# Smaller expert blocks, quarter rows and a third weight slot in a routed decoder layer

## What is computed

```python
def hier_moe(h, w_grp, b_grp, w_exp, b_exp, we_gate, we_up, we_down):
    g_sel = argmax(h @ w_grp + b_grp)                  # one of 4 groups
    top_v, top_i = top_k((h @ w_exp + b_exp)[g_sel], 2)  # two of its 8 experts
    ...
    # rows sorted by expert, padded into blocks; per block of rows xb of expert e:
    #   (silu(xb @ we_gate[e]) * (xb @ we_up[e])) @ we_down[e]
    return segment_sum(y * weight, token)
x = layer_norm(ALPHA * x + g1 * mix, ln1_g, ln1_b)
hf = modulate(x, sh2, sc2)
x = layer_norm(ALPHA * x + g2 * hier_moe(hf, ...), ln2_g, ln2_b)
```

## Time and profile before

| | us |
|---|---|
| median of 3 runs (lowest to highest) | 1522.08 (1512.19 to 1526.45) |
| span of the profiled execution | 1523.0 |
| TensorE busy in it | 1262.4 (83%) |
| VectorE busy | 413.6 (27%) |
| ScalarE busy | 307.3 (20%) |
| bytes moved by DMA | 307.24 MB, 202 GB/s in the mean |

### The profile page before, as it was taken

How to read it: one execution, slowest core, us unless ns; L and a number is a source line. 1 busy time by engine, 2 the same in 40 slices (tenths; PEclk the granted TensorE clock), 3 DMA queues, 4 the chain that set the end, 5 groups by cost and what they waited for, 6 DMA issues and landing times.

```text
span 1523.0 us, 18481 instructions
## 1 busy us (share of the span) xinstructions
PE 1262.4 (83%) x6402; PEld 815.4 (54%) x6403; DVE 413.6 (27%) x704; ACT 307.3 (20%) x433; POOL 127.0 (8%) x203
## 2 busy tenths in 40 slices
PE   3899999999999999999987379798887977788710
PEld 3687878787878888888643223233332332233300
DVE  3326240423332260010386601111111111111156
ACT  3255550410000320000100012121211111111221
POOL 0100000000000000000000111111111111111134
PEclk9899999998878999999998579999998999889965
DMA  8744412124232213413003457996999999999631
GB/s 286 238 171 157 176 56 69 48 72 151 83 110 70 84 56 114 165 56 111 31 15 155 193 194 299 389 348 262 396 397 379 393 367 394 383 378 391 259 119 55
DMA packets 69930, 307.24 MB, mean 202 GB/s; under 512 B 10039, under 2 KB 18744, under 8 KB 56917
## 3 DMA queue, kind: packets, MB, share of 16 engines
q1 hardware_dynamic: 59786, 294.77, 50.5%
q0 software_dynamic: 6272, 10.14, 2.1%
q10 hardware_dynamic: 3820, 1.60, 0.4%
HBM read 298.35 MB, written 18.55 MB: 208 GB/s over the span
## 4 chain that ended last, share of the span: by engine, by line
PE 64%; DMA 18%; DVE 8%; issue 4%; ACT 3%; SPq 2%; ACTq 0%; POOL 0%; POOLq 0%; DVEq 0%; PEldq 0%
PE ps L1482 33%; DMA mem<-in_we_up 13%; PE ps L1750 12%; PE ps L1759 5%; PE ps L1709 3%; DMA mem<-in_w_mod 2%; PE ps L1639 2%; PE ps L1742 2%; PE ps L1636 1%; PE ps L1621 1%; DVE mem L1445 1%; PE ps L1647 1%; DMA mem<-in_we_gate 1%; DVE mem L1444 1%; PE ps L1515 1%
## 5 line engine op out<-in xcount | busy, mean ns | idle before, releaser
L1482 PE MATMUL ps<-mem 128*128 128x260 f32 (+1 forms) x2336 | 546.6, 396 | 10.3 <-ACT mem L813 3.9
L1482 PEld LDWEIGHTS ps<-mem 128*128 128x128 f32 (+1 forms) x2336 | 454.5, 196 | 95.3 <-issue 12.6
L1750 PE MATMUL ps<-mem 128*64 128x512 f32 x1120 | 286.7, 671 | 99.9 <-DMA mem<-in_we_up 78.4
L1750 PEld LDWEIGHTS ps<-mem 128*64 128x64 f32 x1120 | 89.7, 154 | 270.9 <-issue 270.9
L1424 DVE TENSOR_TENSOR mem<-mem,ps 64x512 f32<-64x512 f32 x35 | 24.1, 690 | 431.3 <-ACT mem L1002 431.3
L1759 PE MATMUL ps<-mem 128*64 128x512 f32 x560 | 129.2, 604 | 3.4 <-issue 3.4
L1002 ACT ACT_TABLE_LOAD x35 | 44.9, 1283 | 372.5 <-PE ps L1750 372.5
L1759 PEld LDWEIGHTS ps<-mem 128*64 128x64 f32 x560 | 37.5, 138 | 66.8 <-issue 64.5
L710 POOL DMA_INDIRECT pair_scratch<-mem x35 | 32.7, 934 | 458.2 <-DVE mem L1416 458.2
L1416 DVE COPY mem<-ps 64x512 f32<-64x512 f32 x70 | 48.1, 688 | 78.1 <-PE ps L1759 77.0
L1709 PE MATMUL ps<-mem 128*128 128x512 f32 x128 | 59.8, 628 | 0.0
(11 more groups left out here) (284 smaller groups left out, 988.7 us busy)
## 6 DMA issues: line engine op xcount, KB each, us to landing
mem<-in_we_gate SPq DMA_DIRECT2D x32, 2048.0 KB, 12.0
mem<-in_we_up SPq DMA_DIRECT2D x32, 2048.0 KB, 16.5
mem<-in_we_down SPq DMA_DIRECT2D x32, 2048.0 KB, 8.9
mem<-in_w_in SPq DMA_DIRECT2D x14, 2048.0 KB, 8.5
mem<-in_w_mod SPq DMA_DIRECT2D x12, 2048.0 KB, 12.0
out<-mem SPq DMA_DIRECT2D x13, 512.0 KB, 5.3
mem<-in_state_gla SPq DMA_DIRECT2D x8, 512.0 KB, 3.9
mem<-v_scratch SPq DMA_DIRECT2D x8, 512.0 KB, 4.3
```

The lines of the kernel that those rows point to most:

```text
L1482: ins = pe.matmul(out[0:m, h, 0:HALF], w[:, k, col:col + m], src[:, k, h * HALF:(h + 1) * HALF], start=(k == 0), stop=(k == KD - 1))
L1750: ins = pe.matmul(ps[CAP * q:CAP * q + CAP, 2 + j, :], xT[j][:, k, :], ring[3 * slot + q][:, k, :], start=(k == 0), stop=(k == KD - 1))
```

## The change

- `CAP` goes from 64 to 32 rows per block, the largest number of blocks from 48 to 64. A block's rows lie as quarter rows: partition 32 q + s holds values 256 q to 256 q + 255 of row s. Gather and scatter move 128 quarter rows of 1 KB, with an index for each, instead of 64 rows of 4 KB.
- With 32 stationary columns, gate_up writes four column groups: two halves of gate, two halves of up, each 256 wide. down likewise writes four quarters of the result. The row transposes become 2 of 128 x 128, the activation transposes 2 of 64 x 128, the result copy one of 128 x 256. The routing table is made in four column groups.
- The values of `hf` are stored in a permuted order (so the routing weights are loaded in that order too).
- Weights have three slots (`SLOTS`). To make room, buffers are laid out anew: the matrices of the slots lie at `UNITS`, over memory that the first half has done with. Expert 0 is loaded right after job `pb` 7, gate and up of expert 1 after the last `wo` product, then its down matrix, gate and up of expert 2 when the last logits are done, its down matrix when the first two gathers have landed. In the loop expert n waits for expert n-3.
- The plan has for each block its slot and one load count (two register loads, not three), and TensorE branches over three slots. The register loads stand ahead of the block's waits.
- `ln1_g` and `ln1_b` are loaded by SP just after the modulation rows, not by ACT after `z_ready`; `ln2_g`, `ln2_b` and g2 by POOL after the first two gathers. ACT preloads the table of silu ahead of the loop.

```diff
-CAP = 64
+CAP = 32
+QT = P // CAP
+QD = D // QT
+SLOTS = 3
...
-NBLK = 48
+NBLK = 64
...
-SPLITS = 9
+SPLITS = 17
+UNITS = ((0, 3, 4), (1, 2, 6), (7, 8, 5))
...
-        ring = [area(s * WT, KD, 512) for s in range(6)]
+        ring = [area(s * WT, KD, 512) for s in range(9)]
...
-            sp.dma_start(mod_sb[0:NS, 2 * D:6 * D], mod_dram[0:NS, 2 * D:6 * D]).then_inc(mod_back, 16)
+            sp.dma_start(mod_s[0:NS].rearrange("p v d -> p (v d)"), mod_dram[0:NS, 2 * D:5 * D]).then_inc(mod_back, 16)
+            for v, name in enumerate(("ln1_g", "ln1_b")):
+                sp.dma_start(lnp[:, v, :], t[name][0:1, :].to_broadcast([P, D])).then_inc(lnp_in, 16)
...
-                to = ring[3 * slot + m]
+                to = ring[UNITS[slot][m]]
...
-                    sp.dma_start(to.rearrange("p k n -> p (k n)"), w.rearrange("o (p k) n -> p (o k n)", p=P))\
-                      .then_inc(we_in[3 * slot + m], 16)
+                    sp.dma_start(to.rearrange("p (h a) n -> p h (a n)", h=2),
+                                 w.rearrange("o (h p c) n -> p (o h) (c n)", h=2, c=2)).then_inc(we_in[3 * slot + m], 16)
...
+            sp.wait_ge(job_done, INDEX[("pb", 7)] + 1)
+            for m in range(3):
+                load_expert(0, m, 0)
+            sp.wait_ge(outs_ready, 1)
...
             sp.wait_ge(job_done, INDEX[("wo", ORDER[4])] + 1)
-            load_expert(0, 0, 0)
-            load_expert(0, 1, 0)
-            load_expert(0, 2, 0)
             load_expert(1, 0, 1)
+            load_expert(1, 1, 1)
             store_hf(4)
+            load_expert(1, 2, 1)
+            sp.wait_ge(out_sem, 16 * 4)
+            load_expert(2, 0, 2)
             sp.wait_ge(job_done, INDEX[("lg", ORDER[4])] + 1)
-            load_expert(1, 1, 1)
+            for j in range(2):
+                sp.wait_ge(hf_out[j], 16 * (3 - j))
+            load_expert(2, 1, 2)
             sp.wait_ge(blocks_ready, 1)
             for j in range(2):
                 sp.wait_ge(xg_in[j], 16)
-            load_expert(1, 2, 1)
+            load_expert(2, 2, 2)
...
-                pool.indirect_dma_start(xg[j][0:CAP, :], None, hf_dram,
-                                        bass.IndirectOffsetOnAxis(ap=gidx[j][0:CAP, 0:1], axis=0),
+                pool.indirect_dma_start(xg[j], None, hf_dram.rearrange("t (q d) -> (t q) d", q=QT),
+                                        bass.IndirectOffsetOnAxis(ap=gidx[j][:, 0:1], axis=0),
...
+            sc.preload_act_table(ACT.Silu)
...
-                h = hf[p % 2][0:r, :]
-                link(normalise(h, x, r))
-                link(v.tensor_tensor(h, h, modvec(2, i), ALU.mult))
-                link(v.tensor_tensor(h, h, modvec(1, i), ALU.add))
+                h = hf[p % 2][0:r, :].rearrange("t (k p) -> t p k", k=KD)
+                by_k = lambda a: a.rearrange("t (p k) -> t p k", k=KD)
+                link(normalise(u, x, r))
+                link(v.tensor_tensor(u, u, modvec(2, i), ALU.mult))
+                link(v.tensor_tensor(h, by_k(u), by_k(modvec(1, i)), ALU.add))
...
+                for q in range(QT):
+                    ins = pe.matmul(out[CAP * q:CAP * q + CAP, 0, 0:2 * NBLK], place_oh[0:r, n, :],
+                                    named[0:r, n].rearrange("p b c -> p (b c)"),
+                                    start=(n == 0), stop=(n == 2 * TILES - 1))
...
+                for c in range(2):
+                    ins = pe.transpose(ps[:, j, c * P:(c + 1) * P], xg[j][:, c * P:(c + 1) * P], ident[:])
...
                 for k in range(KD):
-                    for q in range(2):
-                        ins = pe.matmul(ps[CAP * q:CAP * q + CAP, 2 + j, :], xT[j][:, k, :], ring[3 * slot + q][:, k, :],
-                                        start=(k == 0), stop=(k == KD - 1))
+                    for q in range(QT):
+                        w = ring[UNITS[slot][q // 2]]
+                        ins = pe.matmul(ps[CAP * q:CAP * q + CAP, 2 + j, 0:QD], xT[j][:, k, :],
+                                        w[:, k, (q % 2) * QD:(q % 2 + 1) * QD], start=(k == 0), stop=(k == KD - 1))
...
-                lies, in0, in1 = weights_of(i * 2 + j)
-                pe.wait_ge(we_in[2], in0 * 16)
-                pe.wait_ge(we_in[5], in1 * 16)
-                for slot in range(2):
-                    with pe.If(lies < 1 if slot == 0 else lies > 0):
+                pe.wait_ge(y_ready[j], i + 1)
+                for slot in range(SLOTS):
+                    with pe.If(lies == slot):
+                        pe.wait_ge(we_in[3 * slot + 2], turn * 16)
                         down(j, slot)
```

More of the change, by code:

```diff
@@ L210, in build @@
         rms = [area(TB + 2080 + NT * j, NT) for j in range(2)]
[L211 to L223, removed]
+        mod_s = area(6 * WT, 3, D)
+        lnp = area(6 * WT + 3072, 2, D)
+        bc = area(A0, 3, D)
+        hf = [area(A0 + 3072 + 1024 * j, D) for j in range(2)]
+        hfT = [area(A0 + 5120 + 1024 * j, KD, P) for j in range(2)]
+        lt = area(A0 + 7168, D)
+        U = 9 * WT
+        X0 = Z0 + 4160
+        x_tok = area(X0, TILES, D)
+        g2b = area(U, D)
+        ln2 = area(U + 1024, 2, D)
+        xg = [area(U + 3072 + QD * j, QD) for j in range(2)]
+        xT = [area(U + 3584 + QD * j, KD, CAP) for j in range(2)]
+        sg = [area(U + 4096 + QD * j, QD) for j in range(2)]
+        act = [area(U + 4096 + QD * j, QD) for j in range(2)]
+        acT = [area(U + 4608 + P * j, 2, 2, CAP) for j in range(2)]
+        yb = [area(U + 4864 + QD * j, QD) for j in range(2)]
+        assert U + 6336 == X0
         yp = [area(WT + 2048 * i, 2, D) for i in range(TILES)]
         ft = [area(4 * WT + 1024 * j, D) for j in range(TILES)]
-        small = [Z0 + 4160]
+        small = [X0 + TILES * D]
         def keep(*shape):
@@ L264, in build @@
         scan_mask = area(2 * WT + 3080, NT)
-        v_samp = area(2 * WT, D)
         v_samp = keep(D)
+        g2s = v_samp
+        q_base = keep(1)
         rt = [TB]
@@ L293, in build @@
         hits = rtmp(NE)
-        plan_f = rtmp(5)
+        plan_f = rtmp(4)
+        load_no = rtmp(1)
         plan_i = rtmp(6).bitcast(I32)
-        row = rtmp(2)
+        row = rtmp(3)
+        turns = rtmp(10)
         place_no = rtmp(CAP)
@@ L308, in build @@
         iota_i = rtmp(64)
[L312 to L322, removed]
+        idx = area(U + 5376, TW, 2).bitcast(I32)
+        gidx = [area(U + 5508 + j, 1).bitcast(I32) for j in range(2)]
+        sidx = [area(U + 5510 + j, 1).bitcast(I32) for j in range(2)]
+        plan = area(U + 5512, 4 * NBLK + 4).bitcast(I32)
+        BLK_SLOT, BLK_TURN, LD_EXPERT, LD_AFTER = (k * NBLK for k in range(4))
+        N_BLK, N_LD, N_EVEN, N_ODD = (4 * NBLK + k for k in range(4))
+        place_oh = area(U, 2 * TILES, CAP)
+        block_oh = area(U + 320, 2 * TILES, NBLK)
+        named = area(U + 960, 2 * TILES, NBLK, 2)
+        outrow = [area(TB + 2944, D), area(A0 - 1024, D)]
         job_done = sem("job_done")
@@ L403, in build @@
         pair = lambda name: [sem(f"{name}{j}") for j in range(2)]
-        we_in = [sem(f"we_in{s}") for s in range(6)]
+        we_in = [sem(f"we_in{s}") for s in range(3 * SLOTS)]
         gidx_copied = sem("gidx_copied")
@@ L960, in _ @@
             sc.wait_ge(z_ready, KD)
-            for v, name in enumerate(("ln1_g", "ln1_b")):
-                sc.dma_start(lnp[:, v, :], t[name][0:1, :].to_broadcast([P, D])).then_inc(lnp_in, 16)
             await_job(sc, ("wo", 4))
@@ L1386, in _ @@
-            for k in range(2):
-                link(v.tensor_scalar_add(plan_i[:, 2 + k:3 + k], plan_i[:, 0:1], 2 + k))
-            link(v.tensor_single_scalar(plan_i[:, 4:6], plan_i[:, 2:4], 1, ALU.logical_shift_right))
-            link(v.tensor_copy(plan_f[:, 1:3], plan_i[:, 4:6]))
+                link(v.tensor_reduce(into, hits[:], AX, ALU.add))
+            link(v.tensor_scalar_min(plan_f[:, 2:3], plan_f[:, 2:3], float(NE - 1)))
+            link(v.scalar_tensor_tensor(hits[:, 0:10], turns[:], load_no[:, 0:1], ones[:, 0:10], ALU.is_le, ALU.mult))
@@ L1732, in _ @@
             out = start(("plan", 0))
-            for k in range(5):
+            for k in range(4):
                 ins = pe.matmul(out[0:1, 0, k * NBLK:(k + 1) * NBLK], plan_f[:, k:k + 1], ident[:, 0:NBLK],
```

173 lines of the change are left out of this document (86 added, 87 removed).

## The result

The changed kernel takes 1474.06 us (median of 4 runs, 1469.62 to 1480.72) against 1519.5 for the kernel before on the same chip: a ratio of 0.971 (0.968 to 0.9745). Its profiled execution spans 1475.9 us with a mean granted clock of 0.883. The forecast of 1462 us was 12 us (0.8%) low; 1474 lies inside the range and on the predicted side.

The account below looks back on a forecast made before the run. The prediction took the weight stream to pace the expert stage: first product at 879.5, plus stream 490, hole 10, late rows 5, last block 9 and final part 68.7, gives 1462 us; range 1436 to 1500.

Parts of the forecast that it names:

- early blocks take over 9 us: Sign of being wrong, expert loop: the prediction expected blocks near 8 us up to expert 13.
- its lower level: Rival, expert loop: TensorE's clock falls through experts 0 to 13, 14.1 us per block, 1605 us; chance 0.09 with groups.
- First product: Start of the expert blocks: 880.4 us before, less 3.0 and 0.6, plus 1.2, 1.0 and 0.5, gives 879.5.
- The gap: Term of TensorE's block time: waiting for its own sequencer, 1.5 us of 7.8 us per block.
- One of three register loads per block: Edit counted ahead of the first product: one load gone, 0.31 us and two register operations of 0.15, -0.6 us.
- limit of 8.7 us: Block time in the early experts up to which TensorE stays hidden behind the weight stream.
- the rival of rows or holes that pace the early experts: Multi-block stretch at 9.5 to 10 us per block, or stream at 379 GB/s: 1475 to 1500 us, chance 0.17.
- The stream's rate: Term after the first product: 194.6 MB of weights, rows and vectors at 397 GB/s, 490 us.
- 10 + 5 us: Stream losses in the expert stage: start-up hole 10 us (0 to 25), late row gathers 5 us (0 to 17).
- the sum's 88 tiles: Weight tiles left to load at the first product with a third slot, instead of 91.
- The rival that it does nothing: Third slot gives only head start, 16 us for three tiles plus 3, stream at its ceiling: 1503 us, chance 0.04.
- Code fetch: Rival, expert loop: the longer loop does not stay resident, 10.8 us per block, 1518 us, no change; chance 0.05.

## Why the prediction was right, and where its terms were off

**The sign held, and of the mechanism the late half.** Smaller blocks were to let the weights' stream run fuller. They do so from 1150 us on, and not before. The kernel before, then the changed one:

```profile
880.00:1150.00 270.00, 227.27 (x1016) 87.16 (x1018) 33.73 (x49) 48.52 (x68) 38.09 (x67) 0.92 0.85 333
1150.00:1370.00 220.00, 176.47 (x786) 67.29 (x784) 26.85 (x39) 37.10 (x52) 29.86 (x52) 0.90 0.95 382
```

```profile
880.00:1150.00 270.00, 190.10 (x2680) 112.03 (x2676) 22.45 (x53) 27.95 (x81) 65.33 (x106) 0.92 0.83 338
1150.00:1370.00 220.00, 133.47 (x1689) 73.51 (x1682) 13.97 (x33) 17.32 (x50) 40.65 (x66) 0.81 1.01 423
```

Two of the prediction's own signs of being wrong came true: "early blocks take over 9 us" (9.7), and a DMA share near 0.90 (0.91 from the first product to the last weights' landing); the share of 0.97 from 920 us on did not come (0.87 in 950 to 1150). With one load a block the early stretch does fill (416 GB/s, share 1.00 in 950 to 1150), so what was forecast for it is possible, but the changed kernel doesn't reach it. TensorE does not sit at its lower level throughout (granted clock 0.92 and 0.81 above). The last load moves forward (1370.73 us; predicted near 1365, 1425.91 before). Of the 47.0 us between the two profiled spans, 38.3 lie ahead of the last weights' landing (1436.0, now 1397.7), 11.5 between it and the end of the last product (17.5, now 6.0), and the part behind that is 2.8 us longer.

**First product**: predicted 879.5, measured 879.57, with terms that cancel. So close an agreement is luck: the version with 16 KB pieces and the one that keeps registers, with nearly the same code up to there, start it at 874.3 and 874.9 us. The permuted write costs more than the 0 taken: 1.94 us for a tile.

```profile
780.63 1.94 DVE L1316 TENSOR_TENSOR mem<-mem 128x1024 f32<-128x1024 f32 x1
```

That is 0.7 us more than the plain write of a tile before (1.22 us), within the bound of "one more 1.2 us pass". The routing table took 4.65 us, predicted 4.9. The wait for the layer-norm vectors is gone, as predicted.

**TensorE's products**: gate/up 3.66 (3.64), down 1.93 (1.85), row transposes 0.44 (0.45), activation transposes 0.45 (0.4). The row of the 8-column product was the right measure. The estimate from the Trainium skill ("TensorE: Matmul & The Clock Gate", Part 3) was 4.6; its figure for three groups does not carry over to these four.

**The gap is the term that failed.** The sum's 1.5 us (a gap of 1.20 to 1.41, one load less, one branch more) took one gap, ahead of gate/up, from a kernel in which the array's longer products covered the sequencer's other work. The one ahead of down (48.4 us over 45 blocks) was not in the sum at all. "One of three register loads per block" counts gate/up's alone: with down's, the kernel before has six in a block and the changed one four. A block took 9.7 us, not 7.8. In blocks 10 to 27, 1.05 us of the 1.9 are the gap ahead of down, 0.2 the one ahead of gate/up, and 0.6 the gate/ups that ran at a lower clock (six of 17 at 5.35 us), which the sum for these blocks had at nothing. By the prediction's own limit of 8.7 us TensorE then sets the early blocks; the rival of rows or holes that pace the early experts (9.5 to 10 us per block, 1475 to 1500) had the period and nearly the time, but the wrong cause: TensorE waited for a gather once, for 4.3 us, ahead of the first block.

**The stream's rate failed the other way.** 397 GB/s was taken as the ceiling; it was not the engines' limit but their rate in the mix of transfers before, of which the whole rows are a part. At 424, the 194.6 MB take 459 us, 31 less than the 490 of the sum. Against this, the holes were not 10 + 5 us: 950 to 1150 us at 356 lost 200 x (1 - 356/424) = 32 us, 900 to 950 us at 251 lost 20, and the first 20 us (375 GB/s) and the last 28 (344) some 8 more. With 60 - 15 - 31 = 14 us more than the sum's 1384.5, the last tile was due at 1398; it landed at 1397.7, 27 us after its issue (8.9 in the middle before). The last product ended 6 us later, not 9: 1403.7, where 1393.5 was predicted. So 1462 came as near as it did by luck: two errors, of 31 and 45 us, met.

**The third slot** carried the sum's 88 tiles and the belief that "three slots keep two experts queued". In this kernel it is worth 2 us, less than can be told. The rival that it does nothing named the wrong reason, a stream at its ceiling: with a lighter sequencer the slot is worth 18 us.

**Code fetch**: the loop stays resident, as taken; no branch on line 1821 is longer than 0.22 us from 950 to 1150 us. But the first round is not free. Blocks 0 to 3 took 10.9, 14.1, 12.3 and 9.8 us, with branches of 4.3 and 3.1 us; the sum had 6 us for the start, and for the clock alone. The Trainium skill ("Runtime: NRT & Kernel Launch", Instruction fetch mechanics) says that a taken branch out of the resident window stalls for a fetch; the long branches of the first round agree with it, and no later round shows such a stall.

**The end**: from the last product 72.2 us, predicted 68.7. It is 72.0 to 72.6 in all versions of the changed kernel, so it is a property of its last part and not of the stage. ACT starts to weigh at 1411.46, but VectorE only at 1414.16; before, the two starts were 1.18 us apart. Why wasn't settled.

## What to carry to other kernels

When products are cut into more and shorter instructions, sum the sequencer's own work per round (register loads, branches, issues) beside the array's: what hid it here was a number of instructions waiting, and that cover shrank with their length. A rate that a trace shows at a share of 1.00 is the rate of that mix of transfers, not a ceiling. A buffer's worth can't be read in a kernel that is too slow to use it; try it again when the slow thing has been mended.

## What the runs showed of the hardware

A register load on TensorE's sequencer holds it for 0.75 us with its checks. The sequencer issued the 64 weight loads and matmuls of a down product in 0.53 us, 8 ns each; for the 128 of a gate/up it needed 1.43 us with half of the columns and 2.28 with all. Four column groups of 32 overlap as fully as two of 64: 64 matmul records of 128 x 32 by 256 columns take 3.66 us, half of the 7.09 us of 32 records of 64 columns by 512 in two groups before. In the two-slot versions the form in which rows are scattered and gathered went with what all transfers get together: 421 GB/s with quarter rows against 404 with whole ones in 1240 to 1340 us, 423 against 416 in 1150 to 1240, at a full share.
